# First shift and scale read by quarters of the contraction, in turn with the weights of four mixing groups

## The chip, the cores and the metric

The kernel runs on one core of one Trainium2 chip. Its time is the device time of one execution, in microseconds (us). All data are fp32. Every product that is not tiny is made of three fp32r matmuls: an operand is split into a high part and the rest (`w_hi`, `w_lo`; `h_hi`, `h_lo`), and high by high, low by high and high by low are summed in PSUM.

## The reference, cut to what matters

Two transformer blocks, one after the other, on 256 tokens of width 2048. Only the head of the first one is touched:

```python
mod = (c @ w_ada[l] + b_ada[l])[:, None, :]          # c: 1 x 2048, w_ada: 2048 x 12288
shift1, scale1, gate1, shift2, scale2, gate2 = jnp.split(mod, N_MOD, axis=-1)
h = rmsnorm(x, g_pre_mix[l]) * (1.0 + scale1) + shift1
proj = h @ w_in[l]
q_a, k_a, v_a, q_h, f_h, i_h, g_h, gate_a, gate_h = jnp.split(proj, splits, axis=-1)
```

After it come rotary sliding-window attention on `q_a, k_a, v_a`, a recurrence on `q_h, f_h, i_h`, gates, and a feed-forward part. The second block has the same make-up without `mod`.

## The kernel before

**Vectors from `w_ada`.** The 12288 columns of `w_ada` are 24 groups of 512 (`COLS`); groups 0 to 3 are shift1, 4 to 7 scale1, 8 to 11 gate1, 12 to 19 shift2 and scale2, 20 to 23 gate2. One group is 2048 x 512 numbers, read in 4 units of 1 MB (4 row tiles of 128 each). VectorE multiplies each row tile by its number of `c` and adds it to an accumulator of 128 x 512 (L1508, L1515 for groups 0 to 7; `add_mod`, L543 and L545, for the others), and a few matmuls against ones then sum over the 128 partitions.

**The start.** SyncE's queue (SP) loads parameters and x, then the 32 units of groups 0 to 7 into the four buffers of `ada_raw`, each when VectorE is done with what the buffer held. VectorE sums them, two groups at a time; PE sums each over the partitions (L2004) and VectorE adds the bias (L1522). Only when all eight are done do `modulate_dve(0)` and `normed_dve` follow; then x is normalised and turned (`transpose_pe`, "norm0", L711) and shifted, scaled and split into `h_hi` and `h_lo` (`split_dve`, L751, L739). Then the first product can start.

**Products.** `Phase` lists the weights in units of 4 row tiles x 512 columns (1 MB), each unit two halves. The units go through four buffers `raw`; ScalarE makes `w_hi` of each half (L629), VectorE `w_lo` (L641), and PE uses them (`products`; L679, L681, L683 with 512 columns moving, L690, L692, L694 for the transposed groups with 256). There are four slots for halves in `w_hi` and `w_lo`. VectorE and ScalarE work four halves ahead. In `mix_in` the groups 0 and 1 are the attention's q, 2 is k and v (256 columns), 3 and 4 are `q_h`, 5 and 6 `f_h`, 7 and 8 `i_h`, 9 and 10 `g_h`, 11 to 20 the gates with the two projections behind them. `mix_gate` is a loop of three turns of a group of 16 row tiles and one of 8.

**Units of the later `w_ada` groups** (8 to 23) lie between weight units in the same buffers `raw`: `mod=` says how many stand in each group of a phase. Where four are done, `mod_pe` sums over the partitions on PE (L561 and L563, or L556 and L557) and PE waits for that sum; `mod_dve` reads it. In `mix_in` there were 32 such units: 4, 4, 2, 2 in the groups 0 to 3, 4 in group 4, 2 in most up to 13.

**Hooks.** Between the products of two groups stands other work, in program order on each engine: the rotary transposes after group 3 (L2040), the attention's scores, turns and values of four blocks after groups 4 to 7, 5 to 8 and 6 to 9, the turn of its result after group 10 (`att0`), and the recurrence from group 10 on.

## Time and profile before

| what | value |
|---|---|
| time, median of 3 runs (lowest to highest) | 3208.34 us (3204.98 to 3210.74) |
| the profiled execution: span, first to last instruction | 3206.2 us |
| PE, VectorE (DVE), ScalarE (ACT) busy | 90%, 56%, 40% of the span |
| read from HBM | 584.98 MB, 183 GB/s over the span |

The profile is of one execution. Its span leaves out what lies before the first and after the last instruction; the median is 2.1 us above the span, so both stand for the same thing within the spread of the runs. A busy PE is not PE at its peak; the distance between the starts of two matmuls says more. PE is TensorE's matmuls, PEld its weight loads, DVE is VectorE, ACT ScalarE, POOL GpSimd, SP SyncE.

### The profile page before, as it was taken

Reading aid. Unit: us, or ns where it says so; the run is one execution under the profiler, and the core shown is the slowest. Engines: PE = TensorE matmul, PEld = TensorE weight load, DVE = VectorE, ACT = ScalarE, POOL = GpSimd, SP = SyncE. Lnnn points to the kernel's source line nnn. Section 1 sums busy time; section 2 is a strip of 40 time slices with the busy share of each in tenths; the row PEclk is TensorE's granted clock in tenths of the full one; section 3 lists DMA queues with packets and bytes.
Section 4 is the critical chain, followed back from the end, with each engine's and each line's share of the span. In section 5 each row is a group of like instructions: output and inputs, shape, how many; then the busy total and the mean of one; then the engine's idle time right before and its main releaser. Section 6 shows DMA issues by size and latency. Waiting matters only on the chain.

```text
span 3206.2 us, 45676 instructions
## 1 busy us (share of the span) xinstructions
PE 2889.5 (90%) x17826; PEld 2593.6 (81%) x17826; DVE 1805.1 (56%) x2001; ACT 1271.4 (40%) x1439; POOL 234.5 (7%) x161
## 2 busy tenths in 40 slices
PE   1398898889997999999999799998899999999987
PEld 1388776677776999789997799876799988999865
DVE  7885466544586444554446543255466654666444
ACT  0134443433434444333333443353454543444343
POOL 2010011010000100000100000000012210122000
PEclk9998898899998999999999899799999999999999
DMA  8696454434484555665557553343455555555443
GB/s 294 236 327 220 162 178 162 133 112 177 171 313 159 183 183 195 238 223 183 181 183 252 171 184 121 105 148 112 135 183 181 180 188 184 184 183 171 170 162 117
DMA packets 297674, 588.60 MB, mean 184 GB/s; under 512 B 11722, under 2 KB 16830, under 8 KB 296414
## 3 DMA queue, kind: packets, MB, share of 16 engines
q1 hardware_dynamic: 293512, 580.12, 53.6%
q10 hardware_dynamic: 4054, 6.99, 0.6%
q8 instruction: 74, 1.21, 0.2%
q14 instruction: 34, 0.28, 0.0%
HBM read 584.98 MB, written 2.10 MB: 183 GB/s over the span
## 4 chain that ended last, share of the span: by engine, by line
PE 85%; DVE 9%; ACT 3%; issue 2%; DMA 0%; POOL 0%; DVEq 0%; SPq 0%; POOLq 0%; ACTq 0%; PEldq 0%
PE psum L679 13%; PE psum L683 13%; PE psum L690 13%; PE psum L681 13%; PE psum L692 13%; PE psum L694 13%; DVE ada_acc L1515 3%; DVE mod_acc L545 2%; PE bank L711 1%; PE bank L2016 1%; DVE w_lo L641 1%; ACT w_hi L629 1%; ACT junk L788 1%; PE bank L876 0%; PE bank L563 0%
## 5 line engine op out<-in xcount | busy, mean ns | idle before, releaser
L641 DVE TENSOR_TENSOR w_lo<-raw,w_hi 128x1024 fp32r<-128x1024 f32 x916 | 1187.9, 1308 | 1153.4 <-ACT w_hi L629 1145.3
L629 ACT ACTIVATE w_hi<-raw 128x1024 fp32r<-128x1024 f32 x916 | 955.8, 1048 | 1581.9 <-PE psum L683 842.8
L690 PE MATMUL psum<-h_hi,w_hi 128*128 128x256 f32 x3456 | 980.8, 284 | 1.3 <-DVE w_lo L641 0.7
L692 PE MATMUL psum<-h_lo,w_hi 128*128 128x256 f32 x3456 | 979.9, 284 | 0.0
L694 PE MATMUL psum<-h_hi,w_lo 128*128 128x256 f32 x3456 | 979.7, 283 | 0.0
L690 PEld LDWEIGHTS psum<-h_hi,w_hi 128*128 128x128 f32 x3456 | 665.5, 193 | 2.7 <-DVE w_lo L641 1.6
L692 PEld LDWEIGHTS psum<-h_lo,w_hi 128*128 128x128 f32 x3456 | 665.6, 193 | 0.1
L694 PEld LDWEIGHTS psum<-h_hi,w_lo 128*128 128x128 f32 x3456 | 665.5, 193 | 0.0
L679 PE MATMUL psum<-w_hi,h_hi 128*128 128x512 f32 (+2 forms) x1088 | 432.3, 397 | 28.6 <-ACT sig_p L1430 7.8
L681 PE MATMUL psum<-w_lo,h_hi 128*128 128x512 f32 (+2 forms) x1088 | 427.9, 393 | 0.0
L683 PE MATMUL psum<-w_hi,h_lo 128*128 128x512 f32 (+2 forms) x1088 | 427.6, 393 | 0.0
L679 PE MATMUL psum<-w_hi,hid_hi 128*128 128x512 f32 x704 | 280.4, 398 | 1.8 <-DVE w_lo L641 1.8
L681 PE MATMUL psum<-w_lo,hid_hi 128*128 128x512 f32 x704 | 280.4, 398 | 0.0
L683 PE MATMUL psum<-w_hi,hid_lo 128*128 128x512 f32 x704 | 280.3, 398 | 0.0
L679 PEld LDWEIGHTS psum<-w_hi,h_hi 128*128 128x128 f32 x1088 | 214.4, 197 | 77.2 <-issue 18.3
L683 PEld LDWEIGHTS psum<-w_hi,h_lo 128*128 128x128 f32 x1088 | 214.3, 197 | 42.7
L681 PEld LDWEIGHTS psum<-w_lo,h_hi 128*128 128x128 f32 x1088 | 214.8, 197 | 41.0
L545 DVE SCALAR_TENSOR_TENSOR mod_acc<-raw,cols,mod_acc 128x512 f32<-128x512 f32 x240 | 180.8, 754 | 12.0 <-DMA raw<-in_w_ada_dram 0.4
L679 PEld LDWEIGHTS psum<-w_hi,hid_hi 128*128 128x128 f32 x704 | 133.3, 189 | 35.7 <-DVE w_lo L641 3.4
L683 PEld LDWEIGHTS psum<-w_hi,hid_lo 128*128 128x128 f32 x704 | 133.4, 190 | 32.6
L681 PEld LDWEIGHTS psum<-w_lo,hid_hi 128*128 128x128 f32 x704 | 133.3, 189 | 32.3
L2004 PE MATMUL bank<-ones,ada_acc 128*128 128x1 f32 x64 | 14.9, 354 | 99.9 <-DVE ada_acc L1515 58.4
(291 smaller groups left out, 1854.9 us busy)
## 6 DMA issues: line engine op xcount, KB each, us to landing
raw<-in_w_in_dram SPq DMA_DIRECT2D x120, 1024.0 KB, 5.1
raw<-in_w_ffn_in_dram SPq DMA_DIRECT2D x88, 1024.0 KB, 5.0
raw<-in_w_ffn_up_dram SPq DMA_DIRECT2D x88, 1024.0 KB, 5.0
raw<-in_w_ada_dram SPq DMA_DIRECT2D x64, 1024.0 KB, 5.2
raw<-in_w_ffn_out_dram SPq DMA_DIRECT2D x44, 1024.0 KB, 5.1
raw<-in_w_ffn_down_dram SPq DMA_DIRECT2D x44, 1024.0 KB, 5.1
ada_raw<-in_w_ada_dram SPq DMA_DIRECT2D x32, 1024.0 KB, 5.2
raw<-in_w_out_dram SPq DMA_DIRECT2D x32, 1024.0 KB, 5.2
```

Source lines behind the costliest of these rows:

```text
L545: ins = nc.vector.scalar_tensor_tensor(acc, raw[:, j % 4, k, :], cc, acc, ALU.mult, ALU.add)
L629: nc.scalar.activation(w_hi[:, slot, :, 0:ncol], raw[:, rs, 2 * h:2 * h + 2, 0:ncol], ACT.Copy).then_inc(split_hi, inc)
L641: nc.vector.tensor_tensor(w_lo[:, slot, :, 0:ncol], raw[:, rs, 2 * h:2 * h + 2, 0:ncol], w_hi[:, slot, :, 0:ncol].bitcast(F32), ALU.subtra ...
L679: pe.matmul(o, xh, wh[:, 0:ncol], start=first, stop=False, skip_group_check=True)
L681: pe.matmul(o, xh, wl[:, 0:ncol], start=False, stop=False, skip_group_check=True)
L683: mm = pe.matmul(o, xl, wh[:, 0:ncol], start=False, stop=last, skip_group_check=True)
L690: pe.matmul(o, fh, hi[:, k, :], start=first and f % 2 == 0, stop=False, skip_group_check=True)
L692: pe.matmul(o, fh, lo[:, k, :], start=False, stop=False, skip_group_check=True)
L694: mm = pe.matmul(o, fl, hi[:, k, :], start=False, stop=last, skip_group_check=True)
L711: mm = pe.matmul(o, tile, diag[:, t, :], start=(k == 0 and t == 0), stop=(k == 1 and t == 1), skip_group_check=True)
L788: nc.scalar.activation(junk[:], src[:, t, :], ACT.Square, accum_out=stats[:, r, t:t + 1]).then_inc(sem("squares"), 1)
L1515: ins = nc.vector.scalar_tensor_tensor(ada_acc[:, gg, :], unit, cc, ada_acc[:, gg, :], ALU.mult, ALU.add)
```

## The change

The eight groups of shift1 and scale1 are no longer read one after the other over the whole contraction but by quarters of the feature index: quarter q is the columns 512q to 512q + 511 of both, which is all that is needed for row tiles 4q to 4q + 3 of h. A quarter has eight units of 1 MB, each now two transfers of 512 KB (one of shift1, one of scale1), and VectorE adds 128 x 1024 at a time. The row tiles of h of quarter q are then made (`first_h_dve`, `first_h_act`), from an x that was normalised and turned beforehand into `tokbuf`.

The weights of mixing groups 0 to 3 are read by the same quarters (phase `first`), between the units of the next quarter of `w_ada`. The four sums stay open in PSUM over all quarters: two in `psum`, k and v in bank 1, `q_h` in banks 2 and 3. x moves from SP's queue to ScalarE's; the rotary angles move from the start of VectorE's program to the last quarter.

The later `w_ada` units move: none in the groups 0 to 3, two in each of the groups 4 to 10, two each in 13, 15 and 19, and twelve in `mix_gate`, four in each turn with a sum in each. The rotary and attention hooks move by one group, so that the last values stand after group 10, ahead of `att0`. In pieces:

```diff
...
+        if quarters:
+            for k0 in range(0, KD, KU):
+                for g, (kt, cols) in enumerate(groups):
+                    weight_unit(g, k0, kt, cols)
+            self.end = [len(self.halves) - 2 * (len(groups) - 1 - g) for g in range(len(groups))]
+            groups = []
...
-        self.mix_in = Phase(self, 1, [full, full, (KD, 2 * KV_W)] + [full] * 8
+        self.first = Phase(self, 1, [full, full, (KD, 2 * KV_W), full], quarters=True)
+        self.mix_in = Phase(self, 1, [None] * 4 + [full] * 7
                             + [full, half] * (D // COLS) + [full, half],
-                            mod=[4, 4, 2, 2, 4, 2, 2, 2, 2, 2, 2, 2, 0, 2] + [0] * 7)
-        self.mix_gate = Phase(self, D // COLS - 1, [full, half])
+                            mod=[0] * 4 + [2] * 7 + [0, 0, 2, 0, 2, 0, 0, 0, 2, 0])
+        self.mix_gate = Phase(self, D // COLS - 1, [full, half], mod=[2, 2])
...
-        ada_raw = place("ada_raw", 0, [P, 4, KU, COLS])
-        ada_acc = place("ada_acc", 32, [P, 2, COLS])
+        ada_raw = place("ada_raw", 0, [P, 4, 2, 2, COLS])
+        ada_acc = place("ada_acc", 32, [P, 2, 2, COLS])
...
+        def first_products(pe, q, g):
+            ph = plan.first
+            for h in range(2):
+                idx = 2 * (len(ph.groups) * q + g) + h
+                _, slot, inc, m, _, _, _, ncol = ph.half(0, idx)
+                pe.wait_ge(split_lo, 8 + m + 1)
+                for kk in range(2):
+                    k = ph.halves[idx][3] + kk
+                    begin, end = k == 0, k == KD - 1
+                    wh, wl = w_hi[:, slot, kk, :], w_lo[:, slot, kk, :]
+                    if g < 3:
+                        for t in range(TT):
+                            o = psum[g][:, t, :] if g < 2 else bank[:, 1, t * ncol:(t + 1) * ncol]
+                            xh, xl = h_hi[:, k, t * P:(t + 1) * P], h_lo[:, k, t * P:(t + 1) * P]
+                            pe.matmul(o, xh, wh[:, 0:ncol], start=begin and (g < 2 or t == 0), stop=False,
+                                      skip_group_check=True)
...
+                mm.then_inc(w_used, inc)
+        def ada_sum_pe(pe, q):
+            pe.wait_ge(sem("ada_used"), 4 + 8 * (q + 1))
+            pe.wait_ge(bank_free[0], fill("ada", 0, q))
+            for n in range(8):
+                mm = pe.matmul(bank[:, 0, n:n + 1], ada_acc[:, q % 2, n // 4, (n % 4) * P:(n % 4 + 1) * P],
+                               ones[:, 0:1], start=(n == 0), stop=(n == 7), skip_group_check=True)
+            mm.then_inc(bank_full[0], 1)
+        def ada_dve(dve, q, u):
+            n = 8 * q + u
+            acc = ada_acc[:, q % 2]
+            dve.wait_ge(ada_full[u % 4], 32 * (2 * q + u // 4 + 1))
+            if u == 0 and q >= 2:
+                dve.wait_ge(bank_full[0], filled("ada", 0, q - 2))
+            for kk in range(2):
+                k = 2 * u + kk
+                cc = cols[:, ROW["c"] + k:ROW["c"] + k + 1]
+                if k == 0:
+                    ins = nc.vector.tensor_scalar(acc, ada_raw[:, u % 4, kk], cc, None, ALU.mult)
+                else:
+                    if kk:
+                        dve.wait_ge(sem("ada_order"), n + 1)
+                    else:
+                        dve.wait_ge(sem("ada_used"), 4 + n)
+                    ins = nc.vector.scalar_tensor_tensor(acc, ada_raw[:, u % 4, kk], cc, acc,
+                                                         ALU.mult, ALU.add)
+                ins.then_inc(sem("ada_used") if kk else sem("ada_order"), 1)
+        def first_h_dve(dve, chain, q):
+            dve.wait_ge(bank_full[0], filled("ada", 0, q))
+            nc.vector.tensor_tensor(
+                mod_cols[:, 0:2 * KD].rearrange("p (s k) -> p s k", s=2)[:, :, 4 * q:4 * q + 4],
+                bank[:, 0, 0:8].rearrange("p (s k) -> p s k", s=2),
+                bias_cols[:].rearrange("p (s k) -> p s k", s=2)[:, :, 4 * q:4 * q + 4],
+                ALU.add).then_inc(bank_free[0], 1)
+            dve.wait_ge(bank_free[0], emptied("ada", 0, q))
+            at = ROW["g_pre_mix"] + 4 * q
+            chain(nc.vector.scalar_tensor_tensor(
+                a_cols[:, 0, 4 * q:4 * q + 4], mod_cols[:, KD + 4 * q:KD + 4 * q + 4], 1.0,
+                cols[:, at:at + 4], ALU.add, ALU.mult))
+            if q:
+                dve.wait_ge(sem("first_lo"), q)
+            else:
+                for b in range(4):
+                    dve.wait_ge(bank_free[b], emptied("norm0", b, 1))
+            for n in range(4):
+                f = 4 * q + n
+                ins = nc.vector.tensor_scalar(tmp[:, n // 2, n % 2, :], x_t[:, f, :], a_cols[:, 0, f:f + 1],
+                                              mod_cols[:, f:f + 1], ALU.mult, ALU.add)
+            ins.then_inc(sem("first_scaled"), 1)
+            dve.wait_ge(sem("first_scaled"), q + 1)
+            dve.wait_ge(sem("first_hi"), q + 1)
+            nc.vector.tensor_tensor(h_lo[:, 4 * q:4 * q + 4, :], tmp[:].rearrange("p a b t -> p (a b) t"),
+                                    h_hi[:, 4 * q:4 * q + 4, :].bitcast(F32), ALU.subtract
+                                    ).then_inc(sem("first_lo"), 1)
+        def first_h_act(act, q):
+            act.wait_ge(sem("first_scaled"), q + 1)
+            nc.scalar.activation(h_hi[:, 4 * q:4 * q + 4, :], tmp[:].rearrange("p a b t -> p (a b) t"),
+                                 ACT.Copy).then_inc(sem("first_hi"), 1)
...
+            def load_ada(q, u):
+                sp.wait_ge(sem("ada_used"), 8 * q + u + 1)
+                for n in range(2):
+                    sp.dma_start(ada_raw[:, u % 4, :, n, :], cut(w_ada, 2 * u, 2, n * D + q * COLS, COLS)
+                                 ).then_inc(ada_full[u % 4], 16)
+            def load_first(q, g):
+                ph = plan.first
+                j = len(ph.groups) * q + g
+                c0, ncol = (Q0, Q0 + COLS, KV0, QH0)[g], ph.units[j][3]
+                sp.wait_ge(split_lo, 2 * ph.unit_number(0, j) + 2)
+                sp.dma_start(raw[:, j % 4, :, 0:ncol], cut(W_in, q * KU, KU, c0, ncol)
+                             ).then_inc(raw_full[j % 4], 16)
+            for u in range(8):
+                load_ada(0, u)
+            for q in range(1, 4):
+                for u in range(8):
+                    load_ada(q, u)
+                    if u % 2:
+                        load_first(q - 1, u // 2)
+            for g in range(4):
+                load_first(3, g)
...
+                act.dma_start(*PARAMS[i]).then_inc(sem("x_full"), 16)
+            for i in range(N_X, N_ALL):
                 act.dma_start(*PARAMS[i]).then_inc(sem("params"), 16)
+            act.wait_ge(sem("x_full"), 16)
+            squares_act(act, 0, x)
+            for b in range(KD // 2):
+                act.wait_ge(bank_full[b % 4], filled("norm0", b % 4, b // 4))
+                nc.scalar.activation(x_t[:, 2 * b:2 * b + 2, :],
+                                     bank[:, b % 4, :].rearrange("p (k t) -> p k t", k=2), ACT.Copy
+                                     ).then_inc(bank_free[b % 4], 1)
+            ph = plan.first
+            first_h_act(act, 0)
+            for q in range(4):
+                if q:
+                    first_h_act(act, q)
+                for g in range(4):
+                    split_w_hi(act, ph, 0, *first_unit(q, g))
+                    if q == 3 and g > 1:
+                        act.wait_ge(w_used, ph.done(0, g - 2))
+                        nc.scalar.activation(
+                            qk_tok[:, :, 8 * (g - 2):8 * (g - 1), :],
+                            psum[g - 2][:].rearrange("p t (h d) -> p t h d", d=HD),
+                            ACT.Copy, scale=HD ** -0.5).then_inc(psum_free[g - 2], 1)
             act.wait_ge(sem("angles"), 1)
             nc.scalar.activation(trig[:].rearrange("p s t f -> p s (t f)"), rope[:, 5],
                                  ACT.Sin).then_inc(sem("trig"), 1)
+            split_w_hi(act, plan.mix_in, 0, 0, 2)
+            act.wait_ge(w_used, ph.done(0, 2))
...
+            split_w_hi(act, plan.mix_in, 0, 2, 4)
...
+            ph = plan.first
+            for u in range(8):
+                if u == 2:
+                    normed_dve(dve, 0)
+                ada_dve(dve, 0, u)
+            for q in range(1, 4):
+                for u in range(8):
+                    ada_dve(dve, q, u)
+                    if u == 1:
+                        first_h_dve(dve, chain, q - 1)
+                    if u % 2:
+                        split_w_lo(dve, ph, 0, *first_unit(q - 1, u // 2))
+            first_h_dve(dve, chain, 3)
+            for g in range(4):
+                split_w_lo(dve, ph, 0, *first_unit(3, g))
+                if g == 1:
+                    dve.wait_ge(sem("params"), 16 * (N_ALL - N_X))
...
+            split_w_lo(dve, plan.mix_in, 0, 0, 4)
...
+                if 7 <= g < 11:
+                    values_dve(dve, chain, 0, g - 7)
+                if 5 <= g < 9:
+                    softmax_dve(dve, chain, 0, g - 5, sm, band)
...
+                    mod_dve(dve, ph, i, g)
             split_dve(dve, "merged", h_hi, h_lo, KD)
+            dve.wait_ge(bank_free[3], emptied("mod_gate", 3, 2))
+            modulate_dve(1)
...
+            pe.wait_ge(sem("ones_ready"), 1)
+            ada_sum_pe(pe, 0)
+            for n in range(2):
+                pe.wait_ge(psum_free[n], plan.first.free(0, n))
+            for b in range(1, 4):
+                pe.wait_ge(bank_free[b], emptied("norm0", b, 1))
+            for q in range(4):
+                pe.wait_ge(sem("first_lo"), q + 1)
+                for g in range(4):
+                    if q < 3 and g == 3:
+                        ada_sum_pe(pe, q + 1)
+                    first_products(pe, q, g)
             ph = plan.mix_in
-            for g in range(len(ph.groups)):
+            for g in range(4, len(ph.groups)):
...
+                if g == 4:
...
+                mod_pe(pe, ph, i, 1)
...
```

## Rows read from the trace of the kernel before

**Rows 1.** The page: the span, then busy tenths of 40 slices (80 us each).
```profile
span 3206.2 us, 45676 instructions
...
PE   1398898889997999999999799998899999999987
...
DMA  8696454434484555665557553343455555555443
...
```

**Rows 2.** Stretches: busy us of each engine (instructions), clock, DMA share, GB/s.
```profile
...
73.30:100.50 27.20, 3.72 (x16) 3.56 (x16) 23.67 (x34) 0.00 (x0) 0.00 (x0) 1.00 0.92 308
...
148.00:200.00 52.00, 49.69 (x206) 40.81 (x207) 45.41 (x56) 17.55 (x19) 0.00 (x0) 0.92 0.88 303
200.00:240.00 40.00, 39.70 (x314) 39.42 (x313) 29.88 (x34) 16.84 (x23) 13.33 (x12) 0.96 0.93 311
...
```

**Rows 3.** Costliest groups, 0 to 130 us: busy us, mean ns, idle before.
```profile
...
L1515 DVE SCALAR_TENSOR_TENSOR ada_acc<-ada_raw,cols,ada_acc 128x512 f32<-128x512 f32 x120 | 90.4, 753 | 4.3
L2004 PE MATMUL bank<-ones,ada_acc 128*128 128x1 f32 x64 | 14.9, 354 | 99.9 <-DVE ada_acc L1515 58.4 <-DVE mod_cols L1522 41.5
...
```

**Rows 4.** Timeline, 0 to 40 us: start us, us, what.
```profile
...
12.89 0.43 PE L1980 MATMUL bank<-ident,rows 116*128 116x116 f32 x1 [12.89 <-DMA x<-in_x_dram]
...
19.98 1.89 ACT L788 ACTIVATE junk<-x 128x2048 f32<-128x2048 f32 x1
...
21.25 0.49 DVE L1508 TENSOR_SCALAR ada_acc<-ada_raw,cols 128x512 f32<-128x512 f32 x1 [0.33 <-DVE lb L1493]
...
```

**Rows 5.** Timeline, 120 to 180 us: the serial step before the first product.
```profile
...
130.74 8.34 PE L711 MATMUL bank<-diag,x 128*128 128x128 f32 x48 [1.10 <-DVE diag L802]
132.86 0.99 DVE L751 TENSOR_SCALAR tmp<-bank,a_cols,mod_cols 128x256 f32<-128x256 f32 x2 [2.17 <-PE bank L711]
...
148.75 0.77 PE L679 MATMUL psum<-w_hi,h_hi 128*128 128x512 f32 x1 [6.26 <-issue]
...
151.87 0.63 PE L681 MATMUL psum<-w_lo,h_hi 128*128 128x512 f32 x1
...
152.30 0.63 PE L683 MATMUL psum<-w_hi,h_lo 128*128 128x512 f32 x1
...
156.25 0.39 PE L683 MATMUL psum<-w_hi,h_lo 128*128 128x512 f32 x1
...
156.48 0.39 PE L679 MATMUL psum<-w_hi,h_hi 128*128 128x512 f32 x1
...
```

**Rows 6.** Timeline of PE, end of the fourth mixing group.
```profile
...
239.25 0.28 PE L694 MATMUL psum<-h_hi,w_lo 128*128 128x256 f32 x1
...
```

**Rows 7.** Groups, 148 to 240 us, shapes apart.
```profile
...
L641 DVE TENSOR_TENSOR w_lo<-raw,w_hi 128x1024 fp32r<-128x1024 f32 x27 | 33.4, 1270 | 9.1 <-ACT w_hi L629 9.1
L629 ACT ACTIVATE w_hi<-raw 128x1024 fp32r<-128x1024 f32 x27 | 28.0, 1056 | 43.1 <-DMA raw<-in_w_in_dram 24.5 <-PE psum L683 10.5 <-PE psum L694 8.1
...
L641 DVE TENSOR_TENSOR w_lo<-raw,w_hi 128x512 fp32r<-128x512 f32 x8 | 5.5, 691 | 4.9 <-ACT w_hi L629 4.9
...
```

**Rows 8.** DMA issues, 0 to 130 us: KB each, median us to landing.
```profile
...
ada_raw<-in_w_ada_dram SPq DMA_DIRECT2D x32, 1024.0 KB, 5.2
...
```

**Rows 9.** Timeline of SP's queue, 0 to 340 us.
```profile
...
5.30 110.75 SPq L1114 DMA_DIRECT2D ada_raw<-in_w_ada_dram  x32
...
```

**Rows 10.** Waits of PE, 240 to 765 us: total us, times, longest.
```profile
...
PE bank L561 <- DVE mx L845: 8.3, 2, 6.7
PE bank L2016 <- DVE att_lo L762: 7.6, 1, 7.6
...
```

**Rows 11.** Timeline of PE: the first sum of an ada group.
```profile
...
174.22 0.38 PE L561 MATMUL bank<-ones,mod_acc 128*128 128x1 f32 x2 [1.26 <-DVE mod_acc L545]
...
176.39 0.38 PE L563 MATMUL bank<-ones,mod_b 1*128 1x1 f32 x2
...
```

**Rows 12.** Stretches: a turn of the gate loop, a group of mix_out.
```profile
...
787.65:820.65 33.00, 33.00 (x145) 27.06 (x144) 17.85 (x13) 13.64 (x14) 2.40 (x1) 1.00 0.54 191
...
901.40:927.60 26.20, 25.32 (x101) 19.67 (x101) 23.52 (x27) 11.32 (x12) 0.00 (x0) 0.94 1.03 382
...
```

264 lines of the change are left out of this document (114 added, 150 removed).

## The prediction

> **What bounds the kernel now.** I read the page first [rows 1]. PE is busy 1 tenth and 3 tenths in the first two slices of 80 us and 7 to 9 tenths nearly everywhere later, so the kernel is PE's, except for its start. There the DMA engines are at 8 and 6 tenths, and no product runs.
>
> The stretches [rows 2] divide the start. From 73.3 to 100.5 us two groups of `w_ada` pass: 23.67 of 27.2 us busy on VectorE, 308 GB/s. DMA and VectorE are both near their limit, PE is idle. VectorE's work there is one 128x512 step for each row tile, 753 ns each [rows 3], 128 of them; the rest is its wait for PE's sums (1.87 us a group: 14.9 us for eight). The timeline [rows 5] shows the second piece: when the last sum is done, x is turned (130.74) and scaled, and the first product starts at 148.75. The third piece is groups 0 to 3. PE is busy in nearly all of 148 to 240 us, DMA and VectorE too (303 and 311 GB/s) [rows 2]: 14 weight units and 12 of `w_ada` share it. The fourth group's last product ends at 239.5 [rows 6]. That is the mark against which I cost the front: what counts is when the same product ends afterwards, and what the moved work costs behind it.
>
> **The front, part by part.**
>
> *VectorE.* 128 steps of 512 become 64 of 1024. No row shows a 1024 one; from 512 to 1024 the split of the weights goes from 691 to 1270 ns [rows 7], so I take 753 + 579 = 1.33 us. Bounds: 1.27, what the 1024-wide subtraction takes, and 1.51, twice 753. A quarter is 16 x 1.33 = 21.3 us. Its weights are 6 halves at 1.27 and 2 at 0.69 [rows 7], 9.0 us. Its part of h: four scalings of 128x256 at 0.5 [rows 5], ScalarE's 1.06 and a subtraction of 1.27 [rows 7] with VectorE waiting between, and two tiny steps, together 5 us. Sum 35.3 us a quarter.
>
> *DMA.* A quarter is 8 units of `w_ada` and 3.5 of weights, 12.06 MB. At the 308 GB/s of now it is 39.2 us, at the 382 that a stretch of mix_out reaches [rows 12] 31.6. SP issues four units ahead in `ada_raw` and four in `raw`, so waits of VectorE of a few us stop no transfer. The 32 more issues lie in time when SP waits anyway: it needed 110.75 us for 32 issues [rows 9].
>
> *A quarter* thus takes 37 us: VectorE's 35.3 and a little that neither hides. Bounds 34.5 and 42.
>
> *Before the first full quarter.* x no longer stands ahead of `w_ada` in SP's queue, and the parameters' transposes, which began at 12.89 when x had landed [rows 4], no longer wait for it on that queue. The rotary chain that stood before VectorE's first step at 21.25 [rows 4] goes. VectorE starts at about 14. x (2.1 MB) and quarter 0 (8.4 MB) at 308 GB/s are 34 us from 5.3 on [rows 9]; VectorE's 21.3 us and some 3 of waiting for the norm give 38. Quarter 0 is done at 40 (38 to 42). Squares, turning of x (8.34 us of PE [rows 5]) and its copies hide there.
>
> *Last step of `w_ada`:* 40 + 3 x 37, less the last weights' split of 2.5, is 148.5.
>
> *The tail.* Nothing of `w_ada` is left to hide it. PE sums eight columns (twice 1.87 = 3.7 us [rows 3]), VectorE makes the last four tiles of h (5) and splits the first half (1.3): 10 us. PE meanwhile does the `q_h` part of quarter 2. Then it has quarter 3 of all four groups: 48 matmuls at 0.23 (156.25 to 156.48 [rows 5]), 24 of 256 columns and 48 transposed at 0.127 (314 in 40 us [rows 2]), 20.2 us. The halves and the rotary chain that now stands between them are shorter than that on VectorE. I add 2 us for PE on its lower clock after the idle time. 148.5 + 32 = 180.5 against 239.5: **59 us less**. From the bounds: 38 + 103.5 - 2.5 + 29 = 168, or 42 + 126 - 2.5 + 36 = 201.5, so 71.5 to 38 less.
>
> **What comes back behind it.**
>
> *Sums of the later groups.* Behind the mark there were six sums of four units (after groups 3, 4, 6, 8, 10, 13); now there are five in mix_in and three in the gate loop. One is 174.22 to 176.77 on PE [rows 11] and 0.3 for PE's wait for it. In a stretch of mix_out with one sum the granted clock is 0.94 [rows 12], that is 3 us at 1.2 instead of 2.4 GHz, 1.6 us lost. So 4.6 each, and two more are +9.2 us. Bounds 3 and 6 each.
>
> *The gate loop.* A turn is 33.0 us with PE busy throughout and VectorE at 17.85 [rows 12]. Four units add 16 steps at 0.75 [rows 3], 12 us, less 0.3 where a sum begins [rows 4], on VectorE, 29.6 in all, and bring DMA to 10 units, 10.5 MB, 34 us at 308 GB/s against a turn that the sum makes 37.6. The mix_out group, with as many `w_ada` units as weight units, moves 382 GB/s with PE at 25.32 of 26.2 us [rows 12]. I cost the units themselves at nothing, hidden under PE's products. Without that cover it would be 3 us a turn. SP holds back the first unit of a turn until the last turn's sum is done, with two or three weight units already read: hidden too.
>
> *The attention's last values* now stand between group 10 and `att0`. Before they were a group earlier and cost no wait. PE already waits 7.6 us for `att_lo` [rows 10]; VectorE's values (about 0.8), 16 transposes (0.17 each: 48 in 8.34 us [rows 5]) and ScalarE's first copy come after it now instead of before: +4.5 us (bounds 1 and 7). The other hooks keep their waits, such as the 6.7 us for `mx` [rows 10], one group later. VectorE has 3 us more of softmax in front of its forget-gate steps in group 8; PE has four halves ahead, 11 us: nothing.
>
> *Units in 15 and 19 instead of 4 and 11:* +1 us (0 to 4).
>
> Sum: +15 us (8 to 24). **Total: 59 - 15 = 44 us less.** Against the profiled execution's span of 3206.2 that is 3162; with the 2.1 us between it and the median, 3208.3 - 44 = **3164**.
>
> **A rule that speaks against it.** The `w_ada` reads were 1 MB each, 32 in 110.75 us [rows 9], 3.46 us apart, while each took 5.2 to land [rows 8]: they overlap, and what one costs apart from its bytes is hidden. The Trainium skill, DMA: Bandwidth & Descriptors, section Bandwidth, tells to batch transfers to 1 MiB or more, and its section Anatomy of one DMA gives about 2.0 us fixed plus bytes by 436 GB/s. By that, were they not overlapped, a transfer of 512 KB would be 3.2 us, a quarter some 67 us, and the kernel slower. The trace disagrees as to the overlap, at 1 MB; no row shows 512 KB.
>
> **Rivals.**
>
> *Half-size reads cost as much as whole ones* (ends slower). If each transfer of 512 KB holds the queue for the 3.46 us that one of 1 MB holds it now, a quarter is 19.5 x 3.46 = 67.5 us, quarter 0 62: the mark comes at 62 + 202.5 - 3.5 + 32 = 293, and with the 15 behind it the kernel is at 3277. It turns slower when the quarters pass 51 us, which is about 2.5 us for each 512 KB. Against it: the overlap, and the same packets (rows of 512 numbers in both). 4 in 100.
>
> *The quarters take 44 us*: SP's single order, VectorE's and ScalarE's waits for each other add up, since DMA and VectorE both have less than 2 us to spare. For it: VectorE idled 3.5 us in 27.2 already [rows 2]. Time 3164 + 21 = 3185. 15 in 100.
>
> *PE stays on the lower clock in the front.* It works about 20 of 37 us, in bursts. At 1.2 GHz a matmul of 512 columns is 0.43 (151.87 to 152.30 [rows 5]), a quarter with its sum 20.6 + 6 + 12.2 + 3.7 = 42.5 us, more than 37, and the tail 18 longer: 3164 + 16.5 + 18 = 3199. Against it: the clock was 0.92 to 0.96 in the first groups, which had waits as well [rows 2], and an engine that is always behind is always busy. 7 in 100. (The Trainium skill, TensorE: Matmul & The Clock Gate, Part 1, has the half rate as the default that activity lifts; the rows agree in that the first products of all run at 0.43.)
>
> *More comes back behind*: gate turns bound by VectorE and DMA as above, and a late VectorE in the attention: 3 x 3 + 5 more, 3178. 15 in 100.
>
> *The front is shorter*: quarters of VectorE's 34.5 and a tail of 29: 3152. 10 in 100.
>
> The forecast 45 in 100, between 3157 and 3172. 4 in 100 are for what I haven't thought of, half of it slower.
>
> **Range and chances.** From the bounds of both parts: 3208 - 71.5 + 8 = 3145, 3208 - 38 + 24 = 3194. I keep 3145 to 3192. A measurement of this kernel can tell about 0.2%, 6.4 us, from no change. Faster 0.92, within it 0.02, slower 0.06.
>
> **What would show it.** In the profile after: first `w_ada` step on VectorE at 14 us, not 21; steps of 1.33; the last one at about 148; DMA at 310 to 340 GB/s without a hole to there; the last product of the fourth group at about 180; three gate turns of 37 to 38 us; a wait for `att_lo` or values of some 12 us after group 10. The prediction is wrong if VectorE waits for landed reads in the quarters (half-size reads), if PE is what VectorE and ScalarE wait for there (clock, slots), or if the front gives its 59 us and the end moves by much less.

## The result, and the profile after

The changed kernel takes 3133.41 us, the median of four runs (3131.26 to 3137.68), against 3208.04 (3204.98 to 3210.74) for the kernel before on the same chip: ratio 0.977, 95% interval 0.9757 to 0.9784. That is 74.6 us less. Forecast were 44 less, 3164 us, and a range that ended at 3145: the direction was right, the size and the range were wrong. The profiled executions have spans of 3129.5 and 3206.2 us, 76.7 apart; the accounts below are made between these two.

The page after, busy tenths in 40 slices of 78 us, to be held against [rows 1]:

```profile
span 3129.5 us, 45481 instructions
PE 2888.1 (92%) x17826; PEld 2591.9 (83%) x17826; DVE 1773.3 (57%) x1932; ACT 1274.8 (41%) x1445; POOL 227.5 (7%) x161
...
PE   4888888889979999999997999989899999999987
...
DMA  9964544447765556655566553334455555555443
```

PE's busy time has hardly changed, but its first slice stands at 4 tenths instead of 1 and its second at 8 instead of 3, and the DMA engines are at 9 in both. Most of the idle time at the start is gone; the work is the same.

The front by stretches (VectorE's start on each quarter of `w_ada`, the last step's end at 136.2, the mark of the prediction at 165.1):

```profile
core 0: us, PE busy (x) PEld busy (x) DVE busy (x) ACT busy (x) POOL busy (x), PEclk, DMA share, GB/s
40.80:73.40 32.60, 22.32 (x106) 19.23 (x107) 30.62 (x33) 8.11 (x9) 0.00 (x0) 0.76 1.05 385
73.40:105.80 32.40, 25.31 (x130) 21.90 (x130) 30.43 (x32) 8.12 (x9) 0.00 (x0) 0.87 1.05 384
105.80:136.20 30.40, 23.41 (x127) 20.43 (x127) 28.43 (x31) 8.13 (x9) 0.00 (x0) 0.92 1.04 378
136.20:165.10 28.90, 28.89 (x186) 27.00 (x187) 19.68 (x34) 15.47 (x21) 1.88 (x3) 0.94 0.60 192
```

A full quarter takes 32.5 us, not 37. VectorE is busy in 30.5 of it and the DMA engines in all of it, at 385 GB/s; both are at their end, and which of them decides can't be read from this row alone. The DMA engines' 385 GB/s are 12.55 MB in the first of these quarters, half a megabyte more than it needs. The tail behind the last step is 28.9 us, with PE busy in all of it. The timeline has the last products of the fourth group (start, duration):

```profile
164.79 0.28 PE L760 MATMUL bank<-h_hi,w_lo 128*128 128x256 f32 x1
164.91 0.28 PE L719 MATMUL psum<-h_hi,w_hi 128*128 128x256 f32 x1
```

The mark stands at 165.1 us. It stood at 239.5 [rows 6], and was forecast at 180.5.

The work behind the mark, first of the kernel before, then of the kernel after, cut at the same products: the last one of the fourth group, of group 11, of group 19, the first one of group 20, the first one of mix_out, the end.

```profile
239.50:523.70 284.20, 247.02 (x1413) 220.57 (x1411) 163.91 (x251) 114.07 (x174) 13.35 (x5) 0.89 0.54 185
523.70:743.20 219.50, 186.14 (x931) 155.90 (x931) 122.16 (x124) 84.36 (x73) 28.93 (x13) 0.92 0.37 124
743.20:746.60 3.40, 1.74 (x16) 1.51 (x15) 2.05 (x3) 3.31 (x6) 0.00 (x0) 1.00 0.49 188
746.60:875.50 128.90, 119.05 (x513) 97.32 (x513) 62.60 (x53) 49.38 (x52) 11.60 (x6) 0.95 0.55 196
875.50:3206.20 2330.70, 2219.61 (x14314) 2013.27 (x14312) 1265.78 (x1294) 972.78 (x1079) 149.92 (x76) 0.97 0.53 178
```

```profile
165.10:429.60 264.50, 236.16 (x1380) 211.45 (x1379) 150.29 (x244) 115.92 (x177) 16.72 (x15) 0.90 0.54 185
429.60:649.20 219.60, 186.23 (x931) 156.03 (x931) 133.16 (x140) 84.35 (x73) 28.92 (x13) 0.92 0.42 143
649.20:658.90 9.70, 5.93 (x34) 5.56 (x31) 3.87 (x6) 3.92 (x6) 2.08 (x2) 0.71 0.79 282
658.90:800.40 141.50, 131.59 (x560) 108.66 (x561) 90.36 (x101) 48.23 (x50) 9.46 (x4) 0.91 0.71 252
800.40:3129.50 2329.10, 2217.52 (x14315) 2011.66 (x14313) 1265.06 (x1294) 972.47 (x1079) 149.86 (x76) 0.97 0.53 178
```

Line by line: -19.7, +0.1, +6.3, +12.6, -1.6: together 2.3 us less, where 15 more were forecast. So the miss has two halves: 15.4 us in the front (74.4 instead of 59), 17.3 behind it. The new sums cost about what they were to cost, +6.3 in the gap ahead of group 20 and +12.6 in the next line, which holds group 20 and the gate loop; 2.1 of the 12.6 are group 20's products, 13.6 us instead of 11.5, at a granted clock of 0.83 instead of 1.00 behind the longer gap. The -19.7 between groups 4 and 11 wasn't foreseen.

### The profile page after: what moved, and what is told of

It reads as the page before. It is cut to its first block, busy times and chain, and to the rows that moved or that the text cites. A ratio compares the mean times of both kernels' runs of the same rounds, so it can differ in the third digit from the quotient of the medians.

```text
span 3129.5 us, 45481 instructions
## 1 busy us (share of the span) xinstructions
PE 2888.1 (92%) x17826; PEld 2591.9 (83%) x17826; DVE 1773.3 (57%) x1932; ACT 1274.8 (41%) x1445; POOL 227.5 (7%) x161
## 4 chain that ended last, share of the span: by engine, by line
PE 86%; DVE 8%; ACT 3%; issue 2%; DMA 1%; POOL 0%; DVEq 0%; ACTq 0%; POOLq 0%; SPq 0%; PEldq 0%
PE psum L708 13%; PE psum L719 13%; PE psum L723 13%; PE psum L721 13%; PE psum L710 13%; PE psum L712 13%; DVE ada_acc L791 2%; DVE mod_acc L575 1%; PE bank L2146 1%; PE bank L847 1%; DVE w_lo L670 1%; ACT w_hi L658 1%; ACT junk L924 1%; PE bank L1012 0%; DMA gla_gain<-in_gla_norm_w_dram 0%
## 5 line engine op out<-in xcount | busy, mean ns | idle before, releaser
L719 PE MATMUL psum<-h_hi,w_hi 128*128 128x256 f32 x3392 | 961.9, 284 | 1.1 <-DVE w_lo L670 0.8
L721 PE MATMUL psum<-h_lo,w_hi 128*128 128x256 f32 x3392 | 961.2, 283 | 0.0
L723 PE MATMUL psum<-h_hi,w_lo 128*128 128x256 f32 x3392 | 961.2, 283 | 0.0
L708 PE MATMUL psum<-w_hi,h_hi 128*128 128x512 f32 (+1 forms) x992 | 394.9, 398 | 23.1 <-ACT sig_p L1598 7.8
L710 PE MATMUL psum<-w_lo,h_hi 128*128 128x512 f32 (+1 forms) x992 | 391.6, 395 | 0.0
L712 PE MATMUL psum<-w_hi,h_lo 128*128 128x512 f32 (+1 forms) x992 | 391.0, 394 | 0.0
L708 PEld LDWEIGHTS psum<-w_hi,h_hi 128*128 128x128 f32 x992 | 194.4, 196 | 69.1 <-issue 12.1
L712 PEld LDWEIGHTS psum<-w_hi,h_lo 128*128 128x128 f32 x992 | 194.3, 196 | 39.5
L710 PEld LDWEIGHTS psum<-w_lo,h_hi 128*128 128x128 f32 x992 | 194.3, 196 | 37.9
L710 PEld LDWEIGHTS psum<-w_lo,hid_hi 128*128 128x128 f32 x704 | 133.4, 190 | 32.4
L712 PEld LDWEIGHTS psum<-w_hi,hid_lo 128*128 128x128 f32 x704 | 133.3, 189 | 32.5
L847 PE MATMUL bank<-diag,x 128*128 128x128 f32 x320 | 46.4, 315 | 56.4 <-DVE diag L938 54.8
```

Of the source, the lines that this page charges most:

```text
L708: pe.matmul(o, xh, wh[:, 0:ncol], start=first, stop=False, skip_group_check=True)
L710: pe.matmul(o, xh, wl[:, 0:ncol], start=False, stop=False, skip_group_check=True)
L712: mm = pe.matmul(o, xl, wh[:, 0:ncol], start=False, stop=last, skip_group_check=True)
L719: pe.matmul(o, fh, hi[:, k, :], start=first and f % 2 == 0, stop=False, skip_group_check=True)
L721: pe.matmul(o, fh, lo[:, k, :], start=False, stop=False, skip_group_check=True)
L723: mm = pe.matmul(o, fl, hi[:, k, :], start=False, stop=last, skip_group_check=True)
```

## The experiments

Groups keep their numbers of mix_in; a *hook* is the gap on PE between the last product of one group and the first of the next. All medians are of the runs on one chip with the kernel before, whose median there was 3207.3 to 3208.7 us. Two facts are needed to read them. The first `w_ada` step starts anywhere from 17.3 to 20.2 us, in nine kernels that differ in nothing ahead of it but the size of the reads, so the mark is also given from that step: 145.5 us in the kernel after. And the identical work from mix_out to the end took between 2324.6 and 2333.6 us in the profiled executions, so the verdicts go by positions in the trace, and a total within 5 us of another is no evidence.

The positions too are of one execution each. Two kernels below whose front is the same as that of the kernel after, or as that with quarter transfers (the last sum of mix_in earlier, sums away from the scores), have the last step at the same distance from the first (116.5 us) but the mark at 146.9 and 146.8 instead of 145.5. The difference lies in the tail, in which PE is busy throughout in every kernel: it takes 28.9 us where the mean granted clock is 0.94, and 30.3 or 30.4 where it is 0.89.

### What a quarter waits for

**Fewer bytes.** The second transfer of each `w_ada` unit reads only 32 of its 512 columns in quarters 1 to 3; VectorE works on what lies there, so the first scale comes from data that aren't the reference's.

```diff
-                    sp.dma_start(ada_raw[:, u % 4, :, n, :], cut(w_ada, 2 * u, 2, n * D + q * COLS, COLS)
+                    nc_ = 32 if n and q else COLS
+                    sp.dma_start(ada_raw[:, u % 4, :, n, 0:nc_], cut(w_ada, 2 * u, 2, n * D + q * COLS, nc_)
```

> The changed kernel, but in the quarters 1 to 3 the second transfer of each unit of w_ada (the scale1 half) reads 32 columns instead of 512; VectorE multiplies what is left in the buffer, so scale1 is not the reference's in three quarters. DMA's work in a quarter falls from 12.06 MB to 8.1, VectorE's stays. Theory V (VectorE sets the quarter: it is idle 3.6 us in 117 between 19 and 136 us): quarters stay at 32.5 us (31.5 to 33), the time within 3 us of the changed kernel's. Theory D (DMA at 385 GB/s sets it, and VectorE is just dragged along): the quarter falls until VectorE's own work shows, by 2 us or more each, 6 us or more in all. Theory P (VectorE's steps are slower because transfers write the same memory): steps fall below 1.28 us.

Measured: 3127.41 us (3125.99 to 3137.24). Its first two full quarters:

```profile
41.00:73.50 32.50, 22.51 (x107) 19.33 (x108) 30.52 (x33) 8.13 (x9) 0.00 (x0) 0.76 0.88 281
73.50:106.00 32.50, 25.46 (x131) 22.00 (x131) 30.53 (x33) 8.13 (x9) 0.00 (x0) 0.87 0.79 249
```

DMA falls from 385 to 281 and 249 GB/s, the quarters keep their 32.5 us, and the mark stands at 165.2. VectorE's steps keep their 1284 ns, so the bytes read beside them didn't slow them either. In the kernel after, VectorE sets the quarter. Of the 5.2 us between the two spans 4.5 lie behind the start of mix_out.

**Half the steps.** VectorE adds 512 of the 1024 columns in quarters 1 to 3 (the first scale is then not summed there); all bytes are read.

```diff
-                    ins = nc.vector.scalar_tensor_tensor(acc, ada_raw[:, u % 4, kk], cc, acc,
-                                                         ALU.mult, ALU.add)
+                    a_, r_ = (acc[:, 0], ada_raw[:, u % 4, kk, 0]) if q else (acc, ada_raw[:, u % 4, kk])
+                    ins = nc.vector.scalar_tensor_tensor(a_, r_, cc, a_, ALU.mult, ALU.add)
```

> The changed kernel, but in the quarters 1 to 3 all steps of VectorE but the first add only the shift1 half (128x512 instead of 128x1024), so scale1 is not the reference's there. VectorE's work in a quarter falls by 15 x 0.53 = 8 us to about 24, DMA's stays at 12.06 MB, which is 31.3 us at the 385 GB/s of the changed kernel's stretch from 40 to 75 us. Theory V with DMA close behind: the quarter falls only to the 31.3 us of DMA, 1 us each, 3 to 5 us in all. If DMA has room to spare (407 GB/s was seen for a slice of the kernel before): quarters of 29.6, 9 us in all. If PE becomes the bound (19.5 us at the full clock, 40 at the lower one), quarters of 30 to 32 with VectorE waiting for slots.

Measured: 3130.79 us (3127.04 to 3133.76), last step at 129.5, mark at 159.9, 5.2 us before that of the kernel after (4.4 counted from the first step). Windows of two quarters, and VectorE's steps in the first (line, operation, count, busy and mean ns, idle time ahead and its releaser):

```profile
40.80:72.20 31.40, 23.82 (x110) 20.95 (x111) 22.97 (x32) 8.12 (x9) 0.00 (x0) 0.72 1.05 385
72.20:103.50 31.30, 26.82 (x138) 24.02 (x137) 22.88 (x31) 8.13 (x9) 0.00 (x0) 0.83 1.05 385
```

```profile
L792 DVE SCALAR_TENSOR_TENSOR ada_acc<-ada_raw,cols,ada_acc 128x512 f32<-128x512 f32 x16 | 12.0, 751 | 4.2 <-DMA ada_raw<-in_w_ada_dram 3.7
```

VectorE is relieved of 7.6 us and a quarter shortens by 1.2 only: now VectorE waits for the DMA, which moves the 12.06 MB of a quarter in 31.3 us at 385 GB/s. So two limits lie 1.2 us apart. From the first step to the last it is 110.6 us instead of 116.5; the tail is one of the long ones, 30.4 at a granted clock of 0.89.

**The scaling of h on ScalarE.** VectorE's four scalings, and its wait for `h_hi` behind them, go to ScalarE; VectorE takes up `h_lo` two `w_ada` steps later.

```diff
...
-            for n in range(4):
-                f = 4 * q + n
-                ins = nc.vector.tensor_scalar(tmp[:, n // 2, n % 2, :], x_t[:, f, :], a_cols[:, 0, f:f + 1],
-                                              mod_cols[:, f:f + 1], ALU.mult, ALU.add)
...
+                nc.scalar.activation(tmp[:, n // 2, n % 2, :], x_t[:, f, :], ACT.Identity,
+                                     scale=a_cols[:, 0, f:f + 1], bias=mod_cols[:, f:f + 1]
+                                     ).then_inc(sem("first_scaled"), 1)
...
```

> The changed kernel, but the shift and scale of x in the front (4 steps of 128x256 a quarter) run on ScalarE, and VectorE does the third unit's steps of w_ada before it comes back to the low part of h. VectorE loses 1.4 us of work and 1.2 us of waiting a quarter. Theory V (VectorE sets the quarter): quarters of about 30 us, 6 to 8 us less in all by the mark, unless DMA holds them at 31.3, then 3 to 5 us; the tail 0 to 1 us longer. Theory D (DMA sets it): within 2 us of the changed kernel.

Measured: 3128.26 us (3123.8 to 3135.09). Quarters of 31.0, 32.1 and 29.3 us instead of 32.6, 32.4 and 30.4, last step at 133.2 instead of 136.2; VectorE's row of steps now ends in a wait for data:

```profile
L791 DVE SCALAR_TENSOR_TENSOR ada_acc<-ada_raw,cols,ada_acc 128x1024 f32<-128x1024 f32 x16 | 20.5, 1284 | 1.9 <-DMA ada_raw<-in_w_ada_dram 1.3
```

The two full quarters are 31.6 us on average, at 385 GB/s: close to the same limit of 31.3, with all of the reference computed. Of the 3.0 us at the last step only 1.5 are left at the mark, which is 144.0 us behind the first step. The loss isn't the edit's: the tail is 30.4 us, with PE busy in all of it at a granted clock of 0.89, while two kernels below with the same edit have 28.9 at 0.94. The tails of this kernel and of the first of those two:

```profile
133.20:163.60 30.40, 30.39 (x186) 28.50 (x187) 18.33 (x30) 17.55 (x25) 1.82 (x3) 0.89 0.64 208
134.40:163.30 28.90, 28.89 (x186) 26.99 (x187) 18.33 (x30) 17.55 (x25) 1.90 (x3) 0.94 0.64 209
```

Over the three of them the edit brings the last step 2 to 3 us nearer to the first, and the mark 1.5 to 2.6.

**Transfers of a quarter of a megabyte.** Four of 256 KB instead of two of 512 for each unit.

```diff
...
-                for n in range(2):
-                    sp.dma_start(ada_raw[:, u % 4, :, n, :], cut(w_ada, 2 * u, 2, n * D + q * COLS, COLS)
+                for n in range(4):
+                    sp.dma_start(ada_raw[:, u % 4, n // 2, n % 2, :],
+                                 w_ada[:, 2 * u + n // 2, bass.ds(n % 2 * D + q * COLS, COLS)]
```

> The changed kernel with each unit of w_ada read by four transfers of 256 KB instead of two of 512 KB; same bytes, same rows of 512 numbers, 128 transfers instead of 64. Theory O (transfers overlap, four units are outstanding, the cost apart from bytes is hidden): the quarters stay at 32.5 us, the time within 3 us of the changed kernel's. Rival, the one that the prediction gave 4 in 100, in its weak form (each transfer has a cost of its own that counts): 64 more transfers at 0.3 us or more each, 20 us or more slower. SP's issues (0.47 us each) rise to 15 us a quarter plus 2, below the 32.5.

Measured: 3123.97 us (3123.77 to 3132.81). Issues between 30 and 136 us, with KB each and the median time to landing, of the kernel after and of this one, then this one's first full quarter:

```profile
ada_raw<-in_w_ada_dram SPq DMA_DIRECT2D x50, 512.0 KB, 7.9
```

```profile
ada_raw<-in_w_ada_dram SPq DMA_DIRECT2D x96, 256.0 KB, 7.4
```

```profile
38.50:71.20 32.70, 22.51 (x107) 19.33 (x108) 30.55 (x32) 8.11 (x9) 0.00 (x0) 0.76 1.05 384
```

Half the size lands in nearly the same time, at 384 GB/s, and the quarters are the same to 0.2 us. By rate and time to landing (an estimate from these rows) some 3 MB are under way at any time in both, which suggests that the time to landing is mostly a transfer's place among the others. The mark comes 2.2 us earlier, but so does the first step (17.4 us): counted from there it is 145.5, as before. The 9 us that the median gains on the kernel after aren't from this edit: another 4.5 of them lie in the identical work behind mix_out.

### What the work behind the mark waits for

**The moved units alone.** The kernel before, with nothing of the quarters: only the modulation units stand where the change puts them, three of its sums in the gate loop.

```diff
-                            mod=[4, 4, 2, 2, 4, 2, 2, 2, 2, 2, 2, 2, 0, 2] + [0] * 7)
-        self.mix_gate = Phase(self, D // COLS - 1, [full, half])
+                            mod=[0] * 4 + [2] * 7 + [0, 0, 2, 0, 2, 0, 0, 0, 2, 0])
+        self.mix_gate = Phase(self, D // COLS - 1, [full, half], mod=[2, 2])
...
```

> The kernel before with only the later w_ada units moved as in the change: none in groups 0 to 3, two in each of 4 to 10, two in 13, 15 and 19, four in each turn of the gate loop; start and hooks as before. By parts from the two traces: groups 0 to 3 lose 12 units and two sums and become PE's 79 us instead of 91, -12; the sum after group 3 goes, -5; one in group 10 goes, -4; the one after group 19 costs +8; the gate loop +10; the wait for att_lo stays. Sum -3, between -9 and +3. If the gain behind the mark came from the moved units and not from the shifted hooks, it is -10 or more.

Measured: 3188.6 us (3178.65 to 3190.19), ratio 0.9926 (0.9909 to 0.9943): 20 us faster, where some 3 had been expected. In spans it is 17.7 (3206.2 to 3188.5): 9.1 at the mark (230.4), 25.2 between it and the end of group 11, 1.6 and 6.3 and 12.7 given back up to mix_out, and 4.0 in the rest. Where the 25 come from can be read from PE's waits between the mark and the first hooks, first before, then here:

```profile
PE bank L561 <- DVE mx L845: 6.7, 1, 6.7
```

```profile
PE bank L563 <- DVE mx L846: 1.3, 1, 1.3
```

Before, a sum stands behind the first scores in PE's order, and waits 6.7 us for its bank, until VectorE has taken the maximum of the scores. Without a sum there the hook is 1.5 us instead of 12.8, though the next one has 7.1 more. The hook behind group 10 falls from 18.9 to 7.0 us, and PE's wait for `att_lo` in it from 7.6 to 1.7, where the expectation had it stay. In the kernel after, the attention stands a group later and its first scores again have a sum behind them (hook of 12.8). That goes with its gaining 19.7 here and not 25.2; the last experiment takes this sum away.

**Only group 11's units.** The same schedule as before, but the two units of group 11 in group 12. VectorE works four halves ahead, so group 11's units stand before `att_lo` in its order, and group 12's behind.

```diff
-mod=[4, 4, 2, 2, 4, 2, 2, 2, 2, 2, 2, 2, 0, 2]
+mod=[4, 4, 2, 2, 4, 2, 2, 2, 2, 2, 2, 0, 2, 2]
```

> The kernel before, with the two modulation units of group 11 moved to group 12, nothing else; the order of VectorE's steps puts group 11's units ahead of att_lo, group 12's behind it. Theory A (part of the gain behind the mark comes from these two units, which the prediction booked at +1): VectorE is free 6.3 us earlier for att_lo, the 7.6 us wait for att_lo at L2016 falls to 1 to 3 us, and the kernel is 5 to 7 us faster (about 3202). Theory B (att_lo is held up by the scans and the slow splits beside GpSimd, which the two units only overlap): the wait stays above 5 us and the time within 2 us of before. The mark at 239.5 us stays in both.

**Only GpSimd later.** In the kernel before, GpSimd computes four 128x1024 differences from 467.9 to 479.4 us, beside six of VectorE's splits. Here it starts when `att_lo` is done.

```diff
             pool.wait_ge(sem("scanned"), 4)
+            pool.wait_ge(bank_free[3], emptied("att0", 3))
```

> The kernel before, with GpSimd's four level differences (467.9 to 479.4 us) made to wait until att_lo has been read out of bank 3, about 490 us. Theory A (the w_lo splits of 2382 ns instead of 1230 ns are slow because GpSimd works beside them): the splits between 465 and 490 us take 1230 ns, VectorE reaches att_lo 5 to 7 us earlier, the wait for att_lo falls from 7.6 to under 3 us; the stretch up to the start of group 12 is 5 to 7 us shorter, and the later differences may give part of it back in the hook after group 11, where the factors are due. Theory B (the splits are slow for their operands, whatever GpSimd does): they stay at 2382 ns, the wait stays, and the later differences only cost, 0 to 10 us.

**Only the forget gate earlier.** ScalarE's Ln and VectorE's scans one group earlier in the kernel before.

```diff
-                if g == 9:
+                if g == 8:
                     act.wait_ge(sem("f_ready"), 1)
...
```

> The kernel before, unchanged but for the forget gate's steps: VectorE's steps on logf and key after group 7 instead of 8, ScalarE's Ln in group 8 instead of 9, the four scans after group 8 instead of 9. Theory S (PE's wait of 7.6 us for att_lo after group 10 came from the scans: they stood beside the short hook after group 9, where PE goes on after 2.6 us, and VectorE never caught up in group 10): the wait falls to 1 or 2 us and the kernel is 6 to 9 us faster than before. Rival U (the two w_ada units and the splits of group 10 make VectorE late by themselves, scans or not): the wait stays above 5 us and the kernel is within 3 us of before.

Measured: 3203.57 us (ratio 0.9987, 0.9978 to 0.9997), 3204.2 (0.9988, 0.9978 to 0.9998) and 3204.27 (0.9993, 0.9983 to 1.0003). The medians are 3 to 4 us below that of the kernel before, which totals can hardly tell from nothing; the trace can. PE's transposes behind group 10 and what they waited for, in the first and in the second (7.6 us before [rows 10]; 4.5 in the third too):

```profile
L2016 PE MATMUL bank<-qs,key 128*128 128x128 f32 x32 | 3.8, 277 | 1.7 <-DVE att_lo L762 1.7
```

```profile
L2017 PE MATMUL bank<-qs,key 128*128 128x128 f32 x32 | 5.4, 350 | 4.5 <-DVE att_lo L762 4.5
```

And VectorE's splits between 467 and 481 us, before and with GpSimd later:

```profile
L641 DVE TENSOR_TENSOR w_lo<-raw,w_hi 128x1024 fp32r<-128x1024 f32 x6 | 13.9, 2382 | 0.0
```

```profile
L641 DVE TENSOR_TENSOR w_lo<-raw,w_hi 128x1024 fp32r<-128x1024 f32 x6 | 7.1, 1217 | 3.6 <-ACT w_hi L629 3.6
```

The two units are worth 5.9 us of the wait, and the hook shrinks from 18.9 to 11.6: Theory A by the wait, though not by the 5 to 7 us in the total. GpSimd's neighbourhood and the scans are worth 3.1 each, and 4.5 us of waiting lies between the two theories of either experiment. All three made VectorE late, and their shares overlap: they add up to 12.1 us of a wait of 7.6. GpSimd's own operations slow down too, as its rows between 460 and 510 us show, before and with GpSimd later:

```profile
L1897 POOL TENSOR_TENSOR fac<-logf 128x1024 f32<-128x1024 f32 x2 | 5.9, 2948 | 2.6 <-DVE logf L1603 2.6
```

```profile
L1898 POOL TENSOR_TENSOR fac<-logf 128x1024 f32<-128x1024 f32 x2 | 4.0, 1994 | 24.0 <-DVE att_lo L762 24.0
```

The splits are Theory A's, 1217 ns. The expectation of 5 to 7 us for GpSimd was too high: with the splits back at 1217 ns VectorE waits 3.6 us for ScalarE's `w_hi` instead.

**The last sum of mix_in earlier**, and **both small edits**. In the kernel after, the two units of group 19 in group 15, so that the sum stands behind group 15 and not in the gap ahead of group 20.

```diff
-mod=[0] * 4 + [2] * 7 + [0, 0, 2, 0, 2, 0, 0, 0, 2, 0])
+mod=[0] * 4 + [2] * 7 + [0, 0, 2, 0, 4, 0, 0, 0, 0, 0])
```

> The changed kernel, but the two w_ada units of group 19 stand in group 15, which then has four, and the sum that was due after group 19 is due after group 15. Theory B (the sum after group 19 costs 8.4 us because it waits 3.5 us for bank 3, which the split of the recurrence's heads holds, and then runs with what follows at the lower clock): the stretch from group 16's end to the end of mix_in is 8 us shorter again, and group 15 pays 3 to 5 us for the sum; 3 to 6 us faster than the changed kernel. Rival (two more units on VectorE in group 15 hold up the level factors that PE waits 6.8 us for): group 15 gets longer by 6 us or more, no gain in all or a loss.

Measured: 3130.68 us (3129.45 to 3131.11). The gap ahead of group 20 is 3.4 again instead of 9.7, the hook behind group 15 is 19.9 instead of 15.9: 2.3 us by positions. Group 20's products also take 2.1 us less, at the full clock again, but group 16's and the second half of group 19's take 1.6 us more each, at a granted clock of 0.87 instead of 1.00; by the end of the gate loop, 622 us behind the mark in both kernels, nothing is left. Theory B's 3 to 6 us aren't there. With the scaling on ScalarE as well:

> Both edits together: scaling on ScalarE in the front and the last sum after group 15. They lie 400 us apart and should add up: 6 to 13 us faster than the changed kernel, 80 to 88 us faster than before. If they don't add up, one of the single results is noise or the state of the clock behind them.

Measured: 3128.03 us (3124.05 to 3131.24); last step at 134.4, mark 143.5 us behind the first step, mix_out begins 3.4 us earlier than in the kernel after, 1.8 of them gained at the mark. 6 to 13 had been expected, so the two edits add up, but to less. With quarter transfers and the scaling on ScalarE:

> The kernel after, with both edits that shortened the front: the w_ada reads of a quarter in pieces of 256 KB, and the scaling of h on ScalarE. Theory A (the edits take different time: the first brings the first step 2.2 us forward, the second takes 1.4 us from VectorE in each quarter until the transfers' 31.3 us bound it): the last step ends at 131 to 132 us instead of 136.2, the mark stands at 161 instead of 165.1, the time is 3122 to 3126. Theory B (the transfers bound the quarters once VectorE has been relieved, so the first only moves the start): last step at 131 to 133, mark at 162 to 163, and the time as the kernel after within 3 us of 3128, the rest being given back in the stretches at the lower clock.

Measured: 3127.14 us (3122.64 to 3130.37); quarters of 31.7, 32.1 and 29.1, last step at 134.2, mark at 163.1, which is 142.9 behind a first step at 20.2. By mark and median this is Theory B: the scaling alone shortens the quarters, the transfers' size does nothing. The last step is later than either theory had it because the first one is: small transfers come with a first step at 17.4 and 17.3 us in two kernels and at 20.2 here, so the 2.2 us at the start can't be put down to them.

**Sums away from the scores.** On the kernel with quarter transfers:

```diff
-mod=[0] * 4 + [2] * 7 + [0, 0, 2, 0, 2, 0, 0, 0, 2, 0])
+mod=[0] * 4 + [4, 2, 2, 2, 2, 2, 0] + [0, 0, 2, 0, 4, 0, 0, 0, 0, 0])
```

> The kernel with quarter transfers (mark at 163.0, group 11 from 405.8 us, the gate loop to 785.4), with its modulation units at other groups: 4, 2, 2, 2, 2, 2, 0 in groups 4 to 10 instead of 2 in each, and group 19's two in group 15. The sums then stand behind groups 4, 6 and 8 instead of 5, 7 and 9, and behind 15 instead of 19. Theory A (what a sum costs is the wait for its bank: behind the first scores it waits 6.7 us for mx, elsewhere nothing): the hook after group 5 shrinks from 12.9 to some 3 us, the one after group 4 grows by 3, after 15 by 4, after 19 the sum's 8 go: group 11 starts 3 to 8 us earlier, the gate loop ends 6 to 11 us earlier, the time is 3113 to 3119. Theory B (the first scores have to wait for VectorE's work on this group anyway, or four units in group 4 make VectorE late there): group 11 starts within 2 us of 405.8 and the time is 3120 to 3128.

Measured: 3123.03 us (3121.13 to 3127.04), ratio 0.9736 (0.9723 to 0.975). PE's longest waits between 185 and 305 us, with the sums at 5 and 7, then at 4 and 6:

```profile
PE bank L591 <- DVE mx L981: 8.3, 2, 6.7
PE bank L1012 <- DVE tokbuf L1049: 4.1, 1, 4.1
```

```profile
PE bank L2182 <- ACT q_t L1408: 6.4, 1, 6.4
PE bank L1012 <- DVE tokbuf L1049: 4.1, 1, 4.1
```

The wait for `mx` falls from 8.3 to 1.3 and the hook behind group 5 from 12.8 to 1.5 us. But the hook behind group 4, where the sum now stands, grows from 4.4 to 14.1, with a wait for `q_t` of 6.4 instead of 2.3, and that behind group 6 from 5.9 to 11.6. Group 11 starts 2.8 us earlier, the gate loop ends 4.0 earlier (4.0 and 5.2 counted from the mark, which stands 1.2 later here). Theory A's 6 to 11 us at the end of the gate loop aren't there, and group 11 isn't within Theory B's 2 us: the cost of a sum isn't only its own wait, and what is taken from one hook partly shows in the next. This kernel has the lowest median of all, though its interval overlaps that of the kernel with quarter transfers (0.9731 to 0.9765); it does not overlap that of the kernel after (0.9757 to 0.9784).

## Why the prediction was wrong in size

**The start.** Forecast: first step at 14 us, quarter 0 done at 40. Measured 19.6 and 40.8. The first was off: PE's transposes of the parameters still wait for the last of them to land, now until 18.2 us, in the timeline

```profile
18.21 0.85 PE L2132 MATMUL bank<-ident,conv_rows 88*128 88x88 f32 x4 [7.58 <-DMA gla_gain<-in_gla_norm_w_dram]
```

but the 3 us that were booked for the norm didn't show: quarter 0 takes 21.2 us, of which VectorE is busy 20.3. +0.8 in all, two misses that cancel.

**The step that failed first: "A quarter thus takes 37 us".** Three of its numbers were too high. VectorE's sum of 35.3 is 32.5: 30.6 of busy time and the rest idle. Counted from start to start, the sixteen steps take 20.4 us instead of 21.3 (the first of a quarter, a plain multiply, 0.78, the others 1.31 on average instead of 1.33), the weights' splits 8.0 instead of 9.0 (1219 ns each instead of 1270, and their starts nearer still), the part for h 4.1 instead of 5 (its four scalings 1.4 instead of 2). The allowance of 1.7 us for "a little that neither hides" was nothing: the DMA's 31.3 runs under VectorE's 32.5, as the first two experiments show. And the 39.2 us for the DMA at 308 GB/s were read from a stretch in which the mean busy share of the DMA engines was 0.92 [rows 2], where it is 1.05 in the quarters; the 382 GB/s of [rows 12], given as the bound, is what it does. From quarter 0 to the last step: 95.4 us instead of 108.5, **13.1 of the 15.4 us**.

**The tail** is 28.9 instead of 32, with PE busy in all of it. h and the first split of quarter 3 were ready 7.5 us behind the last step instead of 10; PE's eight columns took 1.9 us instead of 3.7. PE came to quarter 3 after 9.2 us, held by what was left of quarter 2, at a granted clock of 0.77; so the lower clock, for which 2 us were added on top, lay inside this time. Quarter 3 itself took 19.7 us instead of 20.2. 3.1 us.

**Behind the mark.** The sums were right: +9.2 forecast. Measured they are -5.2 behind the fourth group, some -3 behind group 10, +6.3 ahead of group 20, +10.5 in the gate loop and the gap behind it, some +9 in all, and 2.1 more in group 20's products; a turn is 38.1 us, forecast 37 to 38:

```profile
711.10:749.20 38.10, 37.24 (x161) 30.59 (x160) 26.73 (x30) 13.57 (x14) 2.37 (x1) 0.96 0.77 275
```

The units themselves are hidden there, as forecast: VectorE at 26.7 of 38.1.

**The step that failed second: "+4.5 us" for `att0`, and "+1 us" for "Units in 15 and 19 instead of 4 and 11".** The wait for `att_lo` did not grow from 7.6 to 12, it went: in the kernel after, PE waits nowhere for `att_lo`. The prediction asked what the attention's order adds to VectorE ahead of it, and not what the change takes away there: two `w_ada` units, 6.0 us of steps. Moved alone they are 5.9 us of that wait. That the rest went with the scans, which in the kernel after have a longer hook to stand in, is argued and not shown; moved alone they are 3.1. The two terms were off by 13.1. Against the moved units alone, the kernel after takes 5.5 us more between the mark and the end of group 11. That is near the 4.5 only as a number: the hooks that hold the last values and `att0`, where the 4.5 were booked, are 10.6 us in the kernel after and 5.3 + 7.0 in the other. The excess lies ahead of them, where the sum again stands behind the first scores. The other 4.0 us are in the products: the same groups took 4 us less at PE, with a mean granted clock of 0.90 instead of 0.89. I can't give a cause for that; the same work behind mix_out varies by 9 us from kernel to kernel.

**The two halves of the gain.** By spans the moved units alone give 17.7 us, and the rest of the change the other 59.0. That this is also the prediction's number for the front is chance: it stood for the mark, and the mark moved by 74.4, of which 9.1 come with the units alone.

**The rivals.** *Half-size reads cost as whole ones*: refuted. Transfers of 512 KB and of 256 KB both run at 384 to 385 GB/s where up to eight or sixteen may be under way. The rule cited there, from the Trainium skill, DMA: Bandwidth & Descriptors, section Bandwidth, on batching to 1 MiB, decides nothing here, as the fixed part of a transfer lies under the others. (That rule and the sum cited beside it, from the section Anatomy of one DMA, rest there on transfers that GpSimd issues; these are SP's, and no run here prices one that stands alone.) *Quarters of 44 us* and *PE on its lower clock*: no; the clock was indeed lower, 0.76 in the first full quarter, with 22.3 of 32.6 us busy, but PE had the room: it was idle in 10 of the 32.6. *More comes back*: no. *The front is shorter*, 3152, was the right side, with 10 in 100, and its quarters of 34.5 were still too long. The range's low end took the best case of the front, 71.5 us, of which the mark beat even that by 2.9, and behind it the least that could come back, 8 us. (The bounds of its terms add up to 7 and 23, not 8 and 24.) That something could be gained there wasn't thought of.
